# Loading and projecting the first feature block in two token halves, on one Trainium2 core

## The chip, the cores and the metric

The kernel runs on one core of one Trainium2 chip. The core has TensorE (PE, the matrix engine, with its weight loads listed apart as PEld), VectorE (DVE), ScalarE (ACT), GpSimd (POOL) and SyncE (SP, which here issues most DMAs). The metric is the device time of one execution in microseconds (us), the median over several executions; lower is better.

## The reference

One inference step of a two-layer decoder, for 1024 prompt tokens and 8 x 4 sample tokens (1056 columns together), model width 1024. Only the first token mixer, a causal convolution module, matters here:

```python
hn = rms_norm(h, norm_mix_pre)
a, g = split(hn @ w_glu + b_glu, 2)     # w_glu is 1024 x 2048
u = a * sigmoid(g)
u_ext = concatenate([prev, u])          # prev: 30 rows of state for each sample
c = depthwise_causal_conv(u_ext, w_dw) + b_dw      # width 31
m = silu(layer_norm(c)) @ w_out + b_out
```

After it come a gated FFN with a depthwise convolution of width 3, a layer with stick-breaking attention (over a paged cache of 4096 positions for the samples), and a second FFN.

## The kernel before

Everything is held feature-major: features on the 128 partitions in KB = 8 blocks, the T = 1056 tokens along the free dimension (TT = 8 prompt tiles of 128 tokens and one sample tile of 32). The order of work on each engine is written out by hand, one function for each engine and stage, and engines wait for each other on counting semaphores; each engine runs its list in order, so an instruction that waits holds all behind it.

Each fp32 product is made of three fp32r products. An operand x is cast to its high part on ACT (`xh`), and DVE subtracts to get the low part (`xl`); a weight tile `raw` gives `whi` (ACT, `split_hi`, L341) and `wlo` (DVE, `split_lo`, L345) in the same way. PE adds whi\*xh, whi\*xl and wlo\*xh in PSUM.

The load stage (`load_sp`, `load_pe`, `load_act`, `load_dve`) does this for all 1056 tokens at once. SP loads the token tiles, the first weight tile, the state rows (`srow`), the FFN state rows (`frow`) and the second weight tile. PE turns each token tile (L394) and DVE copies it out of PSUM to `hT` (L471). ACT squares each tile and takes roots; DVE spreads the inverse roots over a diagonal (L479, L483), PE multiplies by a matrix of 1/D to broadcast them (`scales`, L404), and ACT copies them to `rs` (L448): one half of NH = 528 tokens from the first five tiles, the other when all tiles are in. PE turns the state rows (L425) and the FFN rows (L1397), which ACT copies out (L752, L464). Then, for each feature block k, DVE scales `hT` to `xl32` (L509), ACT casts it to `xh` (L458) and DVE makes `xl` (L506).

The GLU stage (`glu_pe`, `glu_act`, `glu_dve`, ...) goes over eight output blocks m, each with a gate product (b = 0) and a value product (b = 1). Block 0 is `first_pair` (L633): its contraction steps k are taken as the operands come, the value two steps behind the gate:

```python
                for k in range(KB + 2):
                    if k < KB:
                        block(0, k)
                    if k >= 2:
                        block(1, k - 2)
```

Each step is nine matmuls of 352 columns. `quad_taps_spread` (L601, L605) follows, then blocks 1 to 7 (L566, and L587 for the last block in halves). ACT reads a block's gate through a sigmoid (L800) and its value (L808). For each of blocks 0 to 6 DVE forms u (L901), sums 29 taps of the convolution in place (L916) and joins the tap sums that PE made (L941); ACT makes the first two taps (L823, L824) and, ahead of them in block 0, the convolution's weight matrices (`quad_weights`, L745, 32 small instructions). `last_gate` (L818) is block 7's sigmoid.

## Time and profile before

| | before |
|---|---|
| median of 3 executions | 3124.04 us (3123.03 to 3125.28) |
| the profiled execution, its own time | 3125.5 us |
| its span | 3123.8 us |
| mean granted TensorE clock | 0.995 |
| PE busy | 3082.4 us (99%) |
| DVE busy | 1982.5 us (63%) |
| ACT busy | 1380.9 us (44%) |
| DMA, mean over the span | 171 GB/s |

Times in the trace count from the start of the span. "Busy" of PE is modelled for pipelined matmuls: one matmul's duration overlaps the next, so the pace is read from starts, not from durations. The profiled execution took 1.7 us more than its span and 1.5 us more than the median.

### The profile page before, as it was taken

The page shows a single profiled execution, that of the slowest core. Times are in us where ns is not written, and L with a number is a line of the kernel's source. Part 1 is how long each engine was busy: PE and PEld are TensorE (multiplying, and loading weights), DVE is VectorE, ACT ScalarE, POOL GpSimd, SP SyncE. Part 2 cuts the span into 40 slices and gives each one's busy share as a digit, 9 for nine tenths or more (in the row PEclk, how much of TensorE's full clock was granted, in tenths as well). Part 3 has the DMA queues.
Part 4 walks back from the last instruction along what each step waited for, and adds up shares of the span by engine and source line. Part 5 has one row for each costly group of instructions (what it writes and reads, how often), then busy time and mean ns, then how long its engine had stood idle before and what let it go on. Part 6 is the DMA issues. An engine that isn't in the chain of part 4 may idle for free.

```text
span 3123.8 us, 68300 instructions
## 1 busy us (share of the span) xinstructions
PE 3082.4 (99%) x27784; PEld 2805.0 (90%) x27784; DVE 1982.5 (63%) x2987; ACT 1380.9 (44%) x2350; POOL 230.0 (7%) x424
## 2 busy tenths in 40 slices
PE   8999999999999999999999999999999999999998
PEld 7988999999999999999666666666799999999998
DVE  6998677644665445543777877777566763465533
ACT  5445633233333333323767677776543223333322
POOL 0211000000000002321111111011000000000000
PEclk9999999999999999999999999999999999999999
DMA  4223233333333335547999999999523333333332
GB/s 129 81 74 82 82 95 88 88 99 109 113 97 87 99 111 175 191 148 222 352 390 383 380 380 386 387 393 371 201 88 89 88 95 101 111 112 86 95 111 84
DMA packets 483067, 535.14 MB, mean 171 GB/s; under 512 B 22673, under 2 KB 401162, under 8 KB 482552
## 3 DMA queue, kind: packets, MB, share of 16 engines
q1 hardware_dynamic: 467254, 482.83, 46.0%
q0 software_dynamic: 15408, 47.75, 4.6%
q8 instruction: 221, 3.62, 0.5%
q14 instruction: 92, 0.75, 0.1%
q10 hardware_dynamic: 92, 0.19, 0.0%
HBM read 486.90 MB, written 33.95 MB: 167 GB/s over the span
## 4 chain that ended last, share of the span: by engine, by line
PE 88%; DVE 8%; ACT 2%; issue 2%; DMA 1%; SPq 0%; DVEq 0%; POOL 0%; ACTq 0%; POOLq 0%
PE PS L1103 60%; PE PS L2168 8%; PE PS L2204 4%; PE PS L2181 4%; DVE mT L916 4%; PE PS L2219 3%; PE PS L2229 2%; PE PS L2238 2%; DVE wlo L345 1%; PE PS L2190 1%; PE PS L633 1%; ACT whi L341 1%; PE PS L1714 1%; PE PS L986 0%; PE PS L677 0%
## 5 line engine op out<-in xcount | busy, mean ns | idle before, releaser
L345 DVE TENSOR_TENSOR wlo<-raw,whi 128x1024 fp32r<-128x1024 f32 x368 | 450.4, 1224 | 574.7 <-ACT whi L341 561.4
L341 ACT CAST whi<-raw 128x1024 fp32r<-128x1024 f32 x368 | 386.1, 1049 | 963.3 <-PE PS L1103 923.6
L1103 PE MATMUL PS<-xfh,whi 128*128 128x264 f32 (+1 forms) x3072 | 631.1, 287 | 0.9 <-DVE wlo L345 0.9
L1103 PE MATMUL PS<-xfl,whi 128*128 128x264 f32 (+1 forms) x3072 | 625.4, 285 | 0.0
L1103 PE MATMUL PS<-xfh,wlo 128*128 128x264 f32 (+1 forms) x3072 | 624.0, 284 | 0.0
L1103 PEld LDWEIGHTS PS<-xfh,whi 128*128 128x128 f32 x3072 | 479.3, 188 | 4.5 <-issue 1.7
L1103 PEld LDWEIGHTS PS<-xfl,whi 128*128 128x128 f32 x3072 | 478.9, 188 | 0.0
L1103 PEld LDWEIGHTS PS<-xfh,wlo 128*128 128x128 f32 x3072 | 478.2, 188 | 0.0
L1103 PE MATMUL PS<-pA,whi 128*128 128x264 f32 x2048 | 333.0, 284 | 0.0
L1103 PEld LDWEIGHTS PS<-pA,whi 128*128 128x128 f32 x2048 | 282.4, 188 | 0.4
L2168 PE MATMUL PS<-ident,kr 128*128 128x128 f32 x2048 | 276.6, 276 | 0.2 <-ACT kt L2299 0.2
L2168 PEld LDWEIGHTS PS<-ident,kr 128*128 128x128 f32 x2048 | 225.9, 140 | 46.2 <-issue 45.5
L2379 DVE COPY kt<-PS 128x512 f32<-128x512 f32 x256 | 170.2, 678 | 104.8 <-PE PS L2168 104.3
L1103 PE MATMUL PS<-pA,wlo 128*128 128x264 f32 x1024 | 205.7, 282 | 0.0
L2299 ACT COPY kt<-PS 128x512 f32<-128x512 f32 x256 | 152.2, 595 | 49.7 <-PE PS L2168 46.7
L1519 DVE TENSOR_SCALAR cv<-gx,fT 128x528 f32<-128x528 f32 (+2 forms) x132 | 49.5, 403 | 189.4 <-issue 182.4
L1103 PEld LDWEIGHTS PS<-pA,wlo 128*128 128x128 f32 x1024 | 157.5, 188 | 0.0
L1523 DVE SCALAR_TENSOR_TENSOR cv<-gx,fT,cv 128x528 f32<-128x528 f32 (+2 forms) x264 | 142.4, 581 | 3.1
L2204 PE MATMUL PS<-vr,wT 128*32 128x256 f32 x2048 | 137.5, 385 | 2.8 <-ACT wT L2316 1.5
L916 DVE SCALAR_TENSOR_TENSOR mT<-u,vec,mT 128x513 f32<-128x513 f32 (+1 forms) x203 | 135.9, 749 | 4.4 <-ACT mT L823 4.4
L1461 ACT ACTIVATE gel<-cv 128x528 f32<-128x528 f32 x88 | 56.9, 646 | 184.3 <-DVEq L1530 184.3
L2181 PE MATMUL PS<-kt,qst 128*32 128x512 f32 x1024 | 124.3, 600 | 5.3 <-issue 3.8
(351 smaller groups left out, 5058.9 us busy)
## 6 DMA issues: line engine op xcount, KB each, us to landing
kr<-in_cache_k SPq DMA_DIRECT2D x256, 512.0 KB, 6.5
vr<-in_cache_v SPq DMA_DIRECT2D x256, 512.0 KB, 6.4
raw<-in_ffn_w_gate SPq DMA_DIRECT2D x88, 512.0 KB, 3.8
raw<-in_ffn_w_up SPq DMA_DIRECT2D x88, 512.0 KB, 3.8
raw<-in_ffn_w_down SPq DMA_DIRECT2D x64, 512.0 KB, 4.1
raw<-in_ffn_w_down SPq DMA_DIRECT2D x32, 384.0 KB, 3.3
raw<-in_conv_w_glu SPq DMA_DIRECT2D x16, 512.0 KB, 4.1
raw<-in_conv_w_out SPq DMA_DIRECT2D x16, 512.0 KB, 4.1
```

What stands on the lines that cost most here:

```text
L341: nc.scalar.copy(whi[b][:], raw[b][:]).then_inc(w_hi, 1)
L345: nc.vector.tensor_tensor(wlo[b][:], raw[b][:], whi[b][:].bitcast(F32), ALU.subtract).then_inc(w_lo, 1)
L916: glu_then(nc.vector.scalar_tensor_tensor(out=d, in0=src, scalar=w, in1=d, op0=ALU.mult, op1=ALU.add))
L1103: mm = nc.tensor.matmul(PS[:, s + c, 0:c1 - c0], wt[t % RING][:, kw + k, :], x(k0 + k)[:, c0:c1], start=start and k == 0 and wt is whi and ...
L1523: then(nc.vector.scalar_tensor_tensor(out=d, in0=win(j), scalar=tap, in1=s_, op0=ALU.mult, op1=ALU.add))
L2168: mm = nc.tensor.transpose(PS[:, bank, j * P:(j + 1) * P], kr[slot][:, a * P:(a + 1) * P], ident[:])
L2181: mm = nc.tensor.matmul(PS[32 * g:32 * g + 32, 2, :], qst[:, c // SEQ_CHUNKS, a, :], kt[:, a, :], start=e == 0, stop=e == 1, skip_group_ch ...
L2204: mm = nc.tensor.matmul(PS[32 * g:32 * g + 32, 3, 0:256], wT[c % 2][:, m, 32 * g:32 * g + 32], vr[slot][:, 256 * g:256 * g + 256], start=F ...
L2219: mm = nc.tensor.matmul(PS[:, 4 + hh, 0:w], qp[pr % 2][r, i * P:(i + 1) * P], kp[pr % 2][r, 512 * kc:512 * kc + w], start=True, stop=True)
L2229: mm = nc.tensor.transpose(PS[:, bank, j * P:(j + 1) * P], wq[hh][:, j * P:(j + 1) * P], ident[:])
L2299: nc.scalar.copy(kt[:, 0:4, m * P:(m + 1) * P], PS[:, turn_bank("page", x, 0), :].rearrange("p (a s) -> p a s", a=4)).then_inc(s_ka, 1)
L2379: nc.vector.tensor_copy(kt[:, 4:8, m * P:(m + 1) * P], PS[:, turn_bank("page", x, 1), :].rearrange("p (a s) -> p a s", a=4)).then_inc(s_kd, 1)
```

## The change

Token tiles arrive in the order 0 to 6, samples, 7; the second weight tile is asked for right behind the first, ahead of the state rows. The operands of block 0 are made in two halves of 528 tokens: sixteen scalings, casts and subtractions of 528 columns instead of eight of 1056. Half 0 needs only the first five tiles and the scales made from them; tile 7's copy to `hT` and the second inverse roots stand on DVE between steps 4 and 5 of half 0. `first_pair(h)` makes gate and value of one half with 264-column matmuls (six for each step) in PSUM banks 4h to 4h+3. The second scales product, the two turns of the state rows and the turn of the FFN rows are taken out of the load and put inside `first_pair(0)`. ACT reads block 0 in halves (`first_half`) and its table switch comes later. The small DVE work for the convolution weights (`wz`, `pick4`) moves behind the operands. `quad_taps_spread` uses bank 3 instead of 7. The remaining edits renumber semaphore counts.

```diff
+        X_ORDER = (0, 1, 2, 3, 4, 5, 6, TT, TT - 1)
+
         def load_sp(sp):
-            for t in range(TT):
-                sp.dma_start(xtok[:, t, :], A["x_prompt"][0][t * P:(t + 1) * P, :]).then_inc(ld_x[t], 16)
-            sp.dma_start(xtok[0:NS, TT, :], A["x_sample"].rearrange("b q d -> (b q) d")).then_inc(ld_x[TT], 16)
+            for t in X_ORDER:
+                if t < TT:
+                    sp.dma_start(xtok[:, t, :], A["x_prompt"][0][t * P:(t + 1) * P, :]).then_inc(ld_x[t], 16)
+                else:
+                    sp.dma_start(xtok[0:NS, TT, :], A["x_sample"].rearrange("b q d -> (b q) d")).then_inc(ld_x[TT], 16)
             sp.wait_ge(ld_x[6], 16)
             load_tile(sp, 0, 0, cols(w_glu, KB), KB)
+            load_tile(sp, 1, 1, cols(w_glu, 0), KB)
...
             ffn_rows_dma(sp, 0, frow0)
...
-        X_AFTER = (None, None, None, None, 1, 2, 3, 5, 6)
+        X_BANK = (4, 6, 0, 2, 6, 0, 2, 6, 4)
+        X_AFTER = (None, None, None, None, 1, 2, 3, 4, None)
+
+        def scales_pe(pe, part):
...
-                pe.wait_ge(x_rt, 3 + r)
...
-                        mm = nc.tensor.transpose(PS[:, 4 + 2 * r + k % 4 // 2, c0:c0 + 120], srow[:, j, k * P:(k + 1) * P], ident[0:120, 0:120])
-                mm.then_inc(st_pe, 1)
-            pe.wait_ge(tr_v, TT + 1)
-            ffn_rows_pe(pe, 0, frow0, 3)
+            scales_pe(pe, 0)
+            turned(EARLY + 2)
+            turned(EARLY + 3)
...
-            scales_out(0)
+            for i, t in enumerate(X_ORDER):
+                n = P if t < TT else NS
+                act.wait_ge(ld_x[t], 16)
+                if i == TT:
+                    act.wait_ge(x_sq, i)
+                    scales_out(0)
+                elif i >= 2:
+                    act.wait_ge(x_sq, i - 1)
+                j = i % 2 if i < TT else 1
+                nc.scalar.activation(junk[j][0:n, :], xtok[0:n, t, :], ACT.Square, accum_out=ssum[0:n, t:t + 1]).then_inc(x_sq, 1)
+                for a, b in ((0, EARLY), (EARLY, TT + 1)):
+                    if i == b - 1:
+                        act.wait_ge(x_sq, b)
+                        nc.scalar.activation(std[:, a:b], ssum[:, a:b], ACT.Sqrt, bias=eps_k[:, 0:1], scale=2.0 ** -30).then_inc(x_rt, 1)
+
+            def high(h, k):
+                act.wait_ge(n_t, KB * h + k + 1)
+                c = slice(h * NH, h * NH + NH)
+                nc.scalar.copy(xh[:, k, c], xl32[:, k, c]).then_inc(n_hi, 1)
+
+            split_hi(act, 0, 0, 0)
+            for k in range(KB):
+                if k == KB - 1:
+                    act.wait_ge(tr_pe, TT + 1)
+                high(0, k)
+                if k == 1:
+                    split_hi(act, 1, 0, 1)
+                if k == 5:
+                    scales_out(1)
+            state_rows_out(act, 0)
+            high(1, 0)
+            state_rows_out(act, 1)
+            high(1, 1)
+            act.wait_ge(f_st, 1)
+            nc.scalar.copy(fT[:, :, :], PS[:, 4, 0:19 * FB].rearrange("p (f r) -> p f r", f=FB)).then_inc(f_ft, 1)
+            for k in range(2, KB):
+                high(1, k)
             table("sigmoid_and_others")
-            split_hi(act, 0, 0, 0)
-            scales_out(1)
-            state_rows_out(act, 0)
-            act.wait_ge(g_wz, 2)
-            for k in range(KB):
-                act.wait_ge(n_t, k + 1)
-                nc.scalar.copy(xh[:, k, :], xl32[:, k, :]).then_inc(n_hi, 1)
-                if k == 0:
-                    split_hi(act, 1, 0, 1)
-                if k == 1:
-                    state_rows_out(act, 1)
-                    act.wait_ge(f_st, 1)
-                    nc.scalar.copy(fT[:, :, :], PS[:, 3, 0:19 * FB].rearrange("p (f r) -> p f r", f=FB)).then_inc(f_ft, 1)
 
...
+            turned(EARLY + 2)
...
+            dve.wait_ge(x_rt, 2)
+            dve.wait_ge(x_sq, TT)
+            scaled(0, 0)
+            scaled(0, 1)
+            split_lo(dve, 0, 0)
+            low(0, 0)
+            for k in range(2, KB):
+                scaled(0, k)
+                if k == 3:
+                    split_lo(dve, 1, 1)
+                low(0, k - 1)
+                if k == 4:
+                    turned(EARLY + 3)
+                    inverse_roots(1, EARLY, TT + 1)
+            dve.wait_ge(x_rt, 4)
+            scaled(1, 0)
+            low(0, KB - 1)
+            for k in range(1, KB):
+                scaled(1, k)
+                low(1, k - 1)
+            low(1, KB - 1)
             dve.wait_ge(g_wz, 1)
...
+                    if k == 0 and h == 1:
+                        pe.wait_ge((f_ft, st_a)[b], b + 1)
                     if b == 0:
-                        pe.wait_ge(n_lo, k + 1)
+                        pe.wait_ge(n_lo, KB * h + k + 1)
                     for wt, x in ((whi, xh), (whi, xl), (wlo, xh)):
-                        for c, (c0, w) in enumerate(CH):
-                            mm = nc.tensor.matmul(ps(b, c, w), wt[b][:, k, :], x[:, k, c0:c0 + w],
+                        for c in range(2):
+                            c0 = h * NH + CW2 * c
+                            mm = nc.tensor.matmul(PS[:, 4 * h + 2 * b + c, 0:CW2], wt[b][:, k, :], x[:, k, c0:c0 + CW2],
                                                   start=k == 0 and wt is whi and x is xh, stop=k == KB - 1 and wt is wlo)
                     if k == KB - 1:
-                        mm.then_inc(w_used, 1)
+                        mm.then_inc((g_h0, w_used)[h], 1)
 
                 for k in range(KB + 2):
                     if k < KB:
                         block(0, k)
                     if k >= 2:
                         block(1, k - 2)
-
-            pe.wait_ge(x_rt, 4)
-            first_pair()
+                    if h == 0 and k == 5:
+                        scales_pe(pe, 1)
+                    if h == 0 and k == 7:
+                        state_rows_pe(pe, 0)
+                    if h == 0 and k == 8:
+                        state_rows_pe(pe, 1)
+                if h == 0:
+                    pe.wait_ge(st_a, 1)
+                    ffn_rows_pe(pe, 0, frow0, 4)
+
+            first_pair(0)
+            first_pair(1)
...
+            def first_half(h):
+                c = slice(h * NH, h * NH + NH)
+                if h == 1:
+                    act.wait_ge(w_used, 3)
+                else:
+                    act.wait_ge(g_h0, 2)
+                nc.scalar.activation(two(sig[:, c]), PS[:, 4 * h:4 * h + 2, 0:CW2], ACT.Sigmoid,
+                                     bias=vec[:, 0, V_BGLU + 1:V_BGLU + 2]).then_inc(g_sig, 1)
+                if h == 1:
+                    act.wait_ge(w_used, 4)
+                nc.scalar.activation(two(val[:, c]), PS[:, 4 * h + 2:4 * h + 4, 0:CW2], ACT.Identity,
+                                     bias=vec[:, 0, V_BGLU:V_BGLU + 1]).then_inc(g_ev, 1)
+
+            first_half(0)
             split_hi(act, 2, 1, 0)
-            gate(0)
-            value(0)
...
-            act.wait_ge(st_a, 2)
             act.wait_ge(x_sp, 3)
-            nc.scalar.copy(wq4[:].rearrange("p g m j -> p (g m j)"), PS[:, 7, 0:P]).then_inc(g_wr, 1)
+            nc.scalar.copy(wq4[:].rearrange("p g m j -> p (g m j)"), PS[:, 3, 0:P]).then_inc(g_wr, 1)
             act.wait_ge(cst, 2)
-            nc.scalar.copy(wq7[0:96].rearrange("p g j -> p (g j)"), PS[0:96, 7, P:P + 4 * TAP8])
```

On ACT, in the load stage, this stood before (`xh<-xl` casts of `xl32`; `scaled` is counted up by DVE's scalings, `load_spread` by PE's broadcast products, `load_states_transposed` by PE's turns of the state rows):

```order
L448 COPY rs<-PS 128x528 [waits load_spread]
L719 ACT_TABLE_LOAD
L341 CAST whi_176<-raw_174 128x1024 [waits weights_used,weights_landed0]
L448 COPY rs<-PS 128x528 [waits load_spread]
L752 COPY stA<-PS 128x480 [waits load_states_transposed]
L752 COPY stA<-PS 128x480
L458 CAST xh<-xl_61 128x1056 [waits scaled,glu_paired_taps]
L341 CAST whi_177<-raw_175 128x1024 [waits weights_used,weights_landed1]
L458 CAST xh<-xl_61 128x1056 [waits scaled]
```

and this stands there now:

```order
L466 CAST xh<-xl_61 128x528 [waits scaled] x4
L446 COPY rs<-PS 128x528 [waits load_spread]
L466 CAST xh<-xl_61 128x528 [waits scaled]
L466 CAST xh<-xl_61 128x528 [waits scaled,transposed]
L806 COPY stA<-PS 128x480 [waits load_states_transposed]
L806 COPY stA<-PS 128x480
L466 CAST xh<-xl_61 128x528 [waits scaled]
L806 COPY stA<-PS 128x480 [waits load_states_transposed]
L806 COPY stA<-PS 128x480
L466 CAST xh<-xl_61 128x528 [waits scaled]
L482 COPY fT<-PS 128x418 [waits ffn_rows_transposed]
L466 CAST xh<-xl_61 128x528 [waits scaled] x6
```

The copy of the second scales (L446) now stands between the casts of steps 5 and 6 of half 0, and the copies of the state rows and FFN rows stand around the first two casts of half 1.

On PE, around the second scales product in half 0, now (`scaled_lo` is counted up by DVE when a step's `xl` is made, `load_diagonal` by its spread inverse roots):

```order
L678 MATMUL PS<-xh,whi_177 128x264 x2
L678 MATMUL PS<-xl,whi_177 128x264 x2
L678 MATMUL PS<-xh,wlo_179 128x264 x2
L397 MATMUL PS<-spread,mean_198 128x264 [waits transposes_read_dve,load_diagonal]
L397 MATMUL PS<-spread,mean_198 128x264
L678 MATMUL PS<-xh,whi_176 128x264 [waits scaled_lo]
```

Before, that product (L404), the turns and block 0 stood on PE one after the other. The product now comes after steps 0 to 5 of half 0's gate and 0 to 3 of its value.

On PE, at the seam between the halves, now:

```order
L409 MATMUL PS<-ident,srow 128x120 [waits load_root,state_rows_landed]
L409 MATMUL PS<-ident,srow 128x120 x7
L678 MATMUL PS<-xh,whi_177 128x264 x2
L678 MATMUL PS<-xl,whi_177 128x264 x2
L678 MATMUL PS<-xh,wlo_179 128x264 x2
L1463 MATMUL PS<-ident,frow_62 128x19 [waits ffn_rows_landed0,load_states_read]
L1463 MATMUL PS<-ident,frow_62 128x19 x21
L678 MATMUL PS<-xh,whi_176 128x264 [waits scaled_lo,ffn_rows_read]
```

The turns of the state rows stand before the last two value steps of half 0, the turn of the FFN rows behind them, and half 1's first matmul waits until ACT has copied the FFN rows out (`ffn_rows_read`).

## Rows read from the trace of the kernel before

**Rows 1.** Chain of waits, 0 to 110 us: start, us, what.

```profile
17.14 8.22 DMA sbias<-in_sb_bias
...
25.41 3.46 PE PS L425 x16
28.87 2.46 PE PS L1397 x22
31.33 25.90 PE PS L633 x144
...
68.68 6.72 DVE mT L916 x10
```

**Rows 2.** Windows: stretch, length, busy us of PE, PEld, DVE, ACT, POOL, granted clock, DMA share, GB/s.

```profile
22.00:24.00 2.00, 1.64 (x4) 0.83 (x4) 1.53 (x3) 0.52 (x1) 0.00 (x0) 0.70 1.10 211
...
31.30:36.50 5.20, 5.20 (x18) 4.84 (x18) 5.20 (x6) 3.39 (x5) 0.00 (x0) 0.50 0.33 101
36.50:57.20 20.70, 20.70 (x134) 20.48 (x136) 12.06 (x11) 6.71 (x8) 0.00 (x0) 1.00 0.03 8
237.65:241.28 3.63, 3.63 (x17) 3.63 (x18) 3.55 (x7) 0.54 (x1) 1.71 (x4) 0.53 0.75 203
```

**Rows 3.** Timeline of PE, 0 to 60 us: start, us, what, idle before and its releaser.

```profile
17.25 1.16 PE L404 MATMUL PS<-spread,mean 128*128 128x264 f32 x4 [0.50 <-DVE spread L479]
...
22.36 1.72 PE L404 MATMUL PS<-spread,mean 128*128 128x264 f32 x4 [2.11 <-DVE spread L483]
...
31.26 1.25 PE L633 MATMUL PS<-xh,whi 128*128 128x352 f32 x3
...
41.58 0.65 PE L633 MATMUL PS<-xl,whi 128*128 128x352 f32 x3
...
56.56 0.65 PE L633 MATMUL PS<-xh,wlo 128*128 128x352 f32 x3
```

**Rows 4.** Timeline of DVE, 110 to 420 us: the same step in blocks 1 and 2.

```profile
117.16 0.75 DVE L941 SCALAR_TENSOR_TENSOR mT<-PS,vec,mT 128x512 f32<-128x512 f32 x1
...
145.14 0.75 DVE L941 SCALAR_TENSOR_TENSOR mT<-PS,vec,mT 128x512 f32<-128x512 f32 x1
```

**Rows 5.** Timeline of PE, 225 to 300 us.

```profile
237.65 0.65 PE L587 MATMUL PS<-xh,whi 128*128 128x264 f32 x2 [2.34 <-ACT sig L818]
...
240.74 0.64 PE L587 MATMUL PS<-xl,whi 128*128 128x264 f32 x2
...
263.94 0.41 PE L587 MATMUL PS<-xl,whi 128*128 128x264 f32 x2
...
269.30 0.40 PE L587 MATMUL PS<-xh,wlo 128*128 128x264 f32 x2
```

**Rows 6.** Timeline of ACT, 0 to 110 us.

```profile
20.18 1.28 ACT L719 ACT_TABLE_LOAD   x1
21.48 1.04 ACT L341 CAST whi<-raw 128x1024 fp32r<-128x1024 f32 x1
...
57.25 1.44 ACT L808 ACTIVATE val<-PS,vec 128x352 f32<-128x352 f32 x3 [1.93 <-PE PS L633]
```

**Rows 7.** The tile `raw` (weights as loaded), 0 to 60 us: DMA from issue to landing.

```profile
DMA to landing us min/median/max: 3.8/4.8/9.4
```

**Rows 8.** Groups by form: line, engine, what, shapes, count | busy us, mean ns | idle before.

```profile
L471 DVE COPY hT<-PS 128x1024 f32<-128x1024 f32 x8 | 9.7, 1219 | 8.9 <-PE PS L394 8.6
...
L345 DVE TENSOR_TENSOR wlo<-raw,whi 128x1024 fp32r<-128x1024 f32 x3 | 3.7, 1222 | 6.9 <-ACT whi L341 6.9
...
L448 ACT COPY rs<-PS 128x528 f32<-128x528 f32 x2 | 1.2, 588 | 1.6 <-PE PS L404 1.6
...
L479 DVE TENSOR_TENSOR spread<-ident,std 128x384 f32<-128x384 f32 x1 | 0.6, 559 | 0.0
...
L1055 DVE TENSOR_TENSOR xl<-xl,xh 128x528 fp32r<-128x528 f32 x8 | 5.7, 708 | 4.4 <-ACT xh L1071 4.1
...
L1071 ACT CAST xh<-xl 128x528 fp32r<-128x528 f32 x8 | 5.1, 634 | 0.3
```

More of the change, by code:

```diff
@@ L383, in yoco_step @@
         EARLY = 5
-        X_BANK = (4, 6, 0, 2, 6, 0, 2, 0, 2)
-        X_AFTER = (None, None, None, None, 1, 2, 3, 5, 6)
+        X_BANK = (4, 6, 0, 2, 6, 0, 2, 6, 4)
+        X_AFTER = (None, None, None, None, 1, 2, 3, 4, None)
+        def scales_pe(pe, part):
+            pe.wait_ge(x_dg, part + 1)
+            pe.wait_ge(tr_v, (1, TT)[part])
+            if part == 0:
+                pe.wait_ge(g_wz, 1)
+            for c in (2 * part, 2 * part + 1):
+                mm = nc.tensor.matmul(PS[:, 4 + c, 0:CW2], mean1[:], spread[:, CW2 * c:CW2 * c + CW2], start=True, stop=True)
+            mm.then_inc(x_sp, 1)
@@ new lines, in state_rows_pe @@
+        def state_rows_pe(pe, r):
+            pe.wait_ge(ld_s, 48)
+            if r == 0:
+                pe.wait_ge(tr_v, TT + 1)
+            else:
+                pe.wait_ge(x_rt, 4)
+            for k in range(4 * r, 4 * r + 4):
+                for j in range(2):
+                    c0 = (k % 2) * 240 + j * 120
+                    mm = nc.tensor.transpose(PS[:, 4 + 2 * r + k % 4 // 2, c0:c0 + 120], srow[:, j, k * P:(k + 1) * P], ident[0:120, 0:120])
+            mm.then_inc(st_pe, 1)
@@ L395, in turned @@
                                              xtok[0:n, t, k * P:(k + 1) * P], ident[0:n, 0:n])
                 mm.then_inc(tr_pe, 1)
-            def scales(part):
-                pe.wait_ge(x_dg, part + 1)
-                pe.wait_ge(tr_v, (1, EARLY)[part])
-                if part == 0:
-                    pe.wait_ge(g_wz, 1)
-                for c in (2 * part, 2 * part + 1):
-                    mm = nc.tensor.matmul(PS[:, 4 + c, 0:CW2], mean1[:], spread[:, CW2 * c:CW2 * c + CW2], start=True, stop=True)
-                mm.then_inc(x_sp, 1)
@@ L407, in load_pe @@
             pe.wait_ge(cst, 2)
-            for t in range(EARLY + 1):
-                turned(t)
+            for i in range(EARLY + 1):
+                turned(i)
             pe.wait_ge(ld_v, LD_V)
@@ L493, in load_dve, with scaled, low @@
             turned(EARLY + 1)
+            turned(EARLY + 2)
+            def scaled(h, k):
+                c = slice(h * NH, h * NH + NH)
+                nc.vector.scalar_tensor_tensor(out=xl32[:, k, c], in0=hT[:, k, c], scalar=vec[:, k, V_MIX_PRE:V_MIX_PRE + 1],
+                                               in1=rs[:, c], op0=ALU.mult, op1=ALU.mult).then_inc(n_t, 1)
+            def low(h, k):
+                c = slice(h * NH, h * NH + NH)
+                dve.wait_ge(n_hi, KB * h + k + 1)
+                nc.vector.tensor_tensor(xl[:, k, c], xl32[:, k, c], xh[:, k, c].bitcast(F32), ALU.subtract).then_inc(n_lo, 1)
+            dve.wait_ge(x_rt, 2)
[19 more added lines that the diff above has]
+            low(1, KB - 1)
             dve.wait_ge(g_wz, 1)
```

111 lines of the change are left out of this document (44 added, 67 removed).

## The prediction

> **What bounds the kernel now.** I read the chain of waits over the first 110 us first, to see which engine holds the end of each stretch. The landing of the state rows and the head bias ends at 25.36, PE turns the state rows and the FFN rows, and block 0's 144 matmuls run without a break until 57.23 [rows 1]. So block 0 starts at 31.3 although its operands could have been there before: the turns stand ahead of it, and they wait for a DMA. Then the windows, for TensorE's clock. It falls to 1.2 GHz shortly before 23, when PE had stood nearly idle, and the first 5.2 us of block 0 run at that level; from 36.5 on it is 2.4 GHz [rows 2]. The timeline of PE gives the idle stretch before the fall, 2.11 us, and the pace: from 41.58 to 56.56 lie 31 groups of three 352-column matmuls, so 161 ns each [rows 3].
>
> What must not be overlooked is what carries the time from 57 on. The taps of block 0 on DVE start only at 68.68 [rows 1], 11.45 us behind the end of block 0's product, because ACT has to read the value, cast a weight tile and make 32 tap matrices first. After that DVE repeats a block every 27.98 us (117.16 to 145.14) [rows 4], and at the end of the stage PE stands 2.34 us waiting for a sigmoid that waits for DVE [rows 5]. So the gain or loss of this change is the shift of the end of block 0's product, plus what changes in those 11.45 us. All later work hangs on that DVE chain and moves with it; a shift is kept in full.
>
> **The change, part by part.** I follow the three engines through their new lists, with each time a start of the span plus durations of rows, and look for the end of block 0, which was 57.23.
>
> *Start of half 0.* PE's first scales product ends where it did, about 18.4 [rows 3], and ACT copies it in 0.6 us. ACT then has tile 7's square and a root left; the whi cast, at 21.48 before, had a table load of 1.28 us ahead of it [rows 6] that is now later, so it starts about 20.5. Its DMA, issued at the old place, would have landed by then (it was issued at 15.6, and 4.8 us is the median) [rows 7]. DVE scales two steps (20.5 to 21.2), makes wlo (1.22 us) [rows 8], then xl of step 0, at 23.4. PE starts at **23.5**, 7.8 us sooner.
>
> *Half 0 runs at DVE's pace.* A 528-column subtraction takes 708 ns and starts of neighbours lie some 0.08 closer; with a scaling of like size a step costs 1.30 us on DVE. Up to xl of step 5 there are five such steps, plus a weight subtraction (1.22), tile 7's copy (1.22), and the small root and the spreading (0.56 and its neighbours, some 0.9 together) [rows 8]: ready at 33.1. For its part PE needs 12 matmuls for a step of both products, 1.46 us at 2.4 GHz; the pace of 264-column matmuls is 122 ns there (263.94 to 269.30, 44 of them) and 221 ns at 1.2 GHz (237.65 to 240.74, 14 of them) [rows 5]. I take the first eight us at 1.2 GHz, as PE stood 3.4 us before. This costs little here, since PE waits for DVE anyway (1.1 us before step 2): PE is through its ten blocks at about 35.2.
>
> *First new wait.* Now the second scales product, 1.0 us. ACT's copy of it (0.6) ends at 37.1, and in ACT's list it stands ahead of the casts of steps 6 and 7. DVE has scaled both long before and stands waiting for xh of step 6, from 33.8 to 37.8; xl of step 6 is there at 38.4. PE waits from 36.2 to 38.5: **2.3 us**.
>
> *Second new wait.* Six blocks of half 0 are left (6 x 6 x 0.122 = 4.4), with the two turns of the state rows and that of the FFN rows between and behind. These took 3.46 and 2.46 us at 1.2 GHz [rows 1]; at 2.4 GHz they cost between half and all of that, and I take 2.0 and 1.8, nearer half for the wide ones. So PE is done at 46.7. Half 1 waits until ACT has copied the FFN rows out (0.5 and the latency): **0.85 us**, so it starts at 47.6. Its operands are a close second: ACT's casts of half 1 stand behind these copies, but xl of steps 0 to 2 are ready by 48.6, ahead of their use, and later ones stay ahead. State and FFN rows have landed long before (25.36 for what came before the second weight tile; some 2 us later now, still far ahead of 41).
>
> *Half 1.* 96 matmuls at 122 ns are 11.7 us, and 0.2 for the last one to drain: block 0 ends at **59.5**, 2.3 us later than before. In sum: start 23.5, work 28.2 (192 x 0.122 = 23.4; 1.0; 3.8), waits 1.1 + 2.3 + 0.85, low clock 3.3 and drain 0.2. Before: start 31.3, work 23.2 (144 x 0.161), low clock 2.3 (the 5.2 us took 18 matmuls), the rest gaps and drain. So the head start of 7.8 us is spent on 4.8 us of turns and scales that now lie inside, 4.2 of waits and 1.0 of clock.
>
> *The clock in the first new wait.* A PE idle stretch of 2.11 and one of 2.34 us each ended in the fall to 1.2 GHz [rows 3, 5]. The new one of 2.3 us is of that size. The stretch behind the later one lasted 3.6 us [rows 2]; 16 matmuls of 221 instead of 122 ns make **1.5 us**, and I take it. The bounds are 0, and 2.3 for 5.2 us as at block 0's start.
>
> *Behind block 0.* ACT had three value reads of 352 columns after the last matmul (1.44 us, from 57.25) [rows 6]; now it has one of 528 left, about 0.7. Everything behind it on ACT is the same, so the DVE taps come **0.7 us** sooner after block 0. PE's own part does not gain, so its wait of 2.34 us at the end of the stage shrinks to 1.7; the 1.2 GHz stretch behind it may vanish, worth 0 to 1.6 us; I take 0. The sample tile's earlier place, bank 3, and the renumbered counts cost nothing: PE and DVE wait elsewhere there. `wz` on DVE (three small operations) ends at 55, before anybody asks.
>
> *Splitting the matmuls.* 192 x 122 against 144 x 161 ns is +0.2 us, contained in the sum above. The Trainium skill's page "TensorE: Matmul & The Clock Gate", section "Back-to-back issue gap", speaks against narrower matmuls: it gives a sustained spacing of about 81 ns at 128 columns and 131 ns at 512, so that spacing hardly shrinks with width. By that, interpolated as an estimate, 192 x 99 against 144 x 110 ns is +3.1 us, 2.9 worse than the rows. The trace disagrees with it: 161 ns at 352 columns is already above its figure for 512.
>
> Sum: +2.3 + 1.5 - 0.7 = **+3.1 us**. The profiled execution would take 3125.5 + 3.1 = 3128.6 us (span 3126.9); it lies 1.5 us above the median, so the forecast is 3124.04 + 3.1 = **3127.1 us**. 0.2% is 6.2 us, about what a measurement of this kernel can tell from no change; the forecast is inside it.
>
> **The rivals.** (a) *The clock stays at 2.4 GHz.* Then +1.6, and with the late stretch gone too 0.0: 3124.0 to 3125.6. For it: the gap is just at the size of those that fell, and more work lies around it. (b) *The second weight tile lands late.* A tile took 9.4 us to land at worst [rows 7]; issued at 16.4, it would be there at 25.8 instead of the 22.4 I assume (6 us, between median and worst). It then holds ACT's cast of step 2, and block 0 ends 1.1 us later: 3128.2. (c) *Slower by over 0.2%.* TensorE falls to 1.2 GHz at 36 to 38 us and stays there, since turns did not raise it before: it was at 1.2 GHz all through the 3.46 and 2.46 us of turns and for 5.2 us of matmuls after [rows 1, 2]. Then the six blocks cost 3.6 more, the turns 2.1 and the first 5.2 us of half 1 2.3: together 8.0 on the +1.6 of (a), so +9.6 and 3133.6. It decides from the point where half 1 starts at the low level after turns at the low level. Against: here matmul blocks lie between the turns. (d) *Faster.* ACT and PE do not bite: the waits of 4.2 us and the low clock of 3.3 go, block 0 ends at 52.0, and with 0.7 this is -5.9, with the late stretch -7.5: 3116.5 to 3118.1. Against: the order of ACT's list makes the first wait certain, unless DVE is much faster than its rows. (e) *Each matmul costs the same whatever its width.* The bound is 192 x 161 ns, 7.5 over the sum: 3134.6. Against: the two paces differ as the widths do [rows 3, 5]. The Trainium skill's spacing, above, would be a mild form.
>
> **How the numbers follow.** Forecast 0.48, (a) 0.28, (b) 0.10, (c) 0.09, (d) 0.04, (e) 0.01. The range of 8 in 10 holds the forecast, (a), (b) and their bounds: 3122 to 3131. Faster is (d), 0.04; slower (c), (e), 0.10; within 0.2%: 0.86.
>
> **What would show it.** In the trace after: first 264-column matmul near 23.5; PE idle 2.3 us behind the second scales product, released by DVE's xl, which waited for ACT's cast; a short idle behind the FFN rows' turn, released by ACT's copy; the end of block 0 at 59 to 61; DVE's first tap 10.8 us behind it; blocks on DVE still every 28 us. A block 0 that ends before 55 or after 64 makes the prediction wrong.

## The result, and the profile after

The changed kernel took 3129.97 us (median of 16 runs, 3125.80 to 3133.28), the kernel before 3124.75 us on the same chip (16 runs, 3123.00 to 3128.30): ratio 1.0017, 95% interval 1.0010 to 1.0023. That is 5.2 us slower, where 3.1 was forecast; the time lies in the range given. The profiled execution took 3132.74 us with a span of 3131.0.

The chain of waits of the changed kernel, 0 to 110 us (start, us, what), has both new waits in it:

```profile
17.85 1.17 PE PS L397 x4
...
27.70 8.29 PE PS L678 x48
35.99 0.90 PE PS L397 x4
36.94 0.47 issue
37.41 0.64 ACT xh L466
38.08 0.72 DVE xl L526
38.84 4.72 PE PS L678 x24
...
46.67 1.48 PE PS L1463 x22
48.18 0.52 ACT fT L482
48.74 13.49 PE PS L678 x96
...
72.95 6.73 DVE mT L982 x10
```

The 24 matmuls at 38.84 took 4.72 us and the 96 of half 1 took 13.49; at 122 ns apiece they would be 2.9 and 11.7. The windows (columns as in [rows 2]) say why: TensorE fell to 1.2 GHz behind each of the two waits.

```profile
38.00:40.00 2.00, 1.16 (x7) 1.16 (x8) 1.92 (x3) 0.58 (x2) 0.00 (x0) 0.84 0.01 4
40.00:42.00 2.00, 2.00 (x11) 2.00 (x11) 0.76 (x2) 0.00 (x0) 0.00 (x0) 0.50 0.00 0
42.00:44.00 2.00, 2.00 (x16) 2.00 (x16) 0.00 (x0) 0.00 (x0) 0.00 (x0) 0.81 0.00 0
...
48.00:50.00 2.00, 1.40 (x11) 1.30 (x10) 1.69 (x4) 1.58 (x3) 0.00 (x0) 0.90 0.00 0
50.00:52.00 2.00, 2.00 (x11) 2.00 (x11) 2.00 (x4) 0.66 (x2) 0.00 (x0) 0.50 0.00 0
52.00:54.00 2.00, 2.00 (x14) 2.00 (x14) 2.00 (x4) 1.24 (x2) 0.00 (x0) 0.75 0.00 0
```

On DVE's timeline the taps begin at 72.95 instead of 68.68, 4.3 us later [rows 1], and the blocks still come every 27.98 us (121.42 to 149.40), as in [rows 4].

```profile
72.95 6.73 DVE L982 SCALAR_TENSOR_TENSOR mT<-u,vec,mT 128x513 f32<-128x513 f32 x10 [4.37 <-ACT mT L877]
...
121.42 0.75 DVE L1007 SCALAR_TENSOR_TENSOR mT<-PS,vec,mT 128x512 f32<-128x512 f32 x1
...
149.40 0.75 DVE L1007 SCALAR_TENSOR_TENSOR mT<-PS,vec,mT 128x512 f32<-128x512 f32 x1
```

At the end of the stage the picture is another. The timeline of PE shows the wait for the sigmoid shorter than in [rows 5] (1.60 instead of 2.34), and the clock stayed at 1.00 behind it. But now PE waits for a transfer, the shifted copies of block 7's first half:

```profile
241.95 0.51 PE L631 MATMUL PS<-xh,whi 128*128 128x264 f32 x2 [1.60 <-ACT sig L872]
...
253.38 7.33 PE L731 MATMUL PS<-shifted,quads 128*32 128x264 f32 x128 [1.33 <-DMA shifted<-u]
```

In the kernel before the same taps had no wait (its timeline of PE):

```profile
249.22 7.33 PE L677 MATMUL PS<-shifted,quads 128*32 128x264 f32 x128
```

The low clock had made PE late enough for them. A run described below, e8, shows it: DVE wrote its u at 239.51, where the kernel before has 239.46, the clock stayed at 1.00 behind the wait for the sigmoid, and PE then stood until the same moment for the copies.

```profile
249.28 7.33 PE L680 MATMUL PS<-shifted,quads 128*32 128x264 f32 x128 [1.48 <-DMA shifted<-u]
```

DVE's timeline of the kernel before has this for the first step on the layer norm's mean, from which on all is the same code:

```profile
263.90 2.55 DVE L1038 TENSOR_TENSOR mT<-mT,PS 128x528 f32<-128x528 f32 x4 [3.81 <-PE PS L986]
```

That step starts at 268.07 in the changed kernel, 4.2 us later. From there on single executions differ by some us: the profiled one of the changed kernel ends 7.2 us behind that of the kernel before (3132.74 against 3125.5), 4.2 of which are there at this step.

The traces place most of the other 3.0 us in the layer with attention, in code that the change does not touch. The kernel before had a fall of the clock there which the changed kernel, behind the same wait, had not. PE's timeline, of the kernel before and then of the changed one:

```profile
1493.68 3.42 PE L2181 MATMUL PS<-kt,qst 128*32 128x512 f32 x16 [1.60 <-issue]
```

```profile
1498.23 1.92 PE L2247 MATMUL PS<-kt,qst 128*32 128x512 f32 x16 [1.59 <-issue]
```

Of the fourteen profiles only that one has a fall at this place. At the end of the attention it went the other way. PE of the changed kernel waited for a transfer that PE of the kernel before did not wait for, and its clock was then low for longer (windows of the changed kernel; the kernel before has 0.72 and 1.00 in the same two):

```profile
2221.67 0.64 PE L2270 MATMUL PS<-vr,wT 128*32 128x256 f32 x8 [1.64 <-DMA vr<-in_cache_v]
```

```profile
2225.00:2230.00 5.00, 2.88 (x21) 2.78 (x20) 2.78 (x5) 3.09 (x6) 0.00 (x0) 0.50 0.38 110
2230.00:2235.00 5.00, 5.00 (x28) 5.00 (x28) 5.00 (x9) 3.42 (x7) 0.00 (x0) 0.59 0.39 101
```

On DVE the distance between the two kernels is 2.0 us ahead of this wait (2213.28 and 2215.31, the copies to `aT`), 4.9 us at the first subtractions behind it (2222.70 and 2227.65), and 6.7 us behind the low clock (2267.87 and 2274.61, the same subtraction of a weight tile). Of the other runs only e2 (1.23 us) and e3 (0.41) waited for that transfer; whether the change brings the wait about is not shown. So single profiles are compared up to the step on the mean, and times by their medians.

### The profile page after: what moved, and what is told of

The parts are those of the page before. It is cut to its first block, busy times and chain, and to the rows that moved or that the text cites. A ratio compares the mean times of both kernels' runs of the same rounds, so it can differ in the third digit from the quotient of the medians.

```text
span 3131.0 us, 68420 instructions
## 1 busy us (share of the span) xinstructions
PE 3081.6 (98%) x27832; PEld 2805.8 (90%) x27832; DVE 1985.0 (63%) x3003; ACT 1382.8 (44%) x2356; POOL 230.6 (7%) x424
## 4 chain that ended last, share of the span: by engine, by line
PE 86%; DVE 8%; ACT 2%; issue 2%; DMA 1%; SPq 0%; DVEq 0%; POOL 0%; ACTq 0%; POOLq 0%
PE PS L1169 59%; PE PS L2234 8%; PE PS L2270 4%; PE PS L2247 4%; DVE mT L982 4%; PE PS L2285 3%; PE PS L2295 2%; PE PS L2304 2%; DVE wlo L345 1%; PE PS L678 1%; PE PS L2256 1%; ACT whi L341 1%; PE PS L1780 1%; PE PS L1052 0%; PE PS L731 0%
```

## The experiments

Differences are of medians, against the kernel before on the same chip. "First tap" and "mean step" are the two starts just read, in the one profiled execution; before: 68.68 and 263.90. The kernel before took 3124.19 us beside e1 to e4, 3125.51 beside e5 to e8 and 3123.86 beside e9 to e12 (33 runs each), so the absolute times in the expectations have to be read as differences too.

| run | us | minus before | ratio, 95% interval | first tap | mean step |
|---|---|---|---|---|---|
| changed kernel | 3129.97 | +5.2 | 1.0010 to 1.0023 | 72.95 | 268.07 |
| e1 | 3128.71 | +4.5 | 1.0000 to 1.0018 | 70.62 | 267.96 |
| e2 | 3129.33 | +5.1 | 1.0009 to 1.0027 | 71.29 | 266.17 |
| e3 | 3131.92 | +7.7 | 1.0013 to 1.0032 | 70.40 | 268.64 |
| e4 | 3124.51 | +0.3 | 0.9991 to 1.0009 | 66.94 | 262.28 |
| e5 | 3131.01 | +5.5 | 1.0012 to 1.0030 | 70.69 | 266.09 |
| e6 | 3128.92 | +3.4 | 1.0002 to 1.0020 | 67.99 | 263.05 |
| e7 | 3126.80 | +1.3 | 0.9996 to 1.0014 | 66.00 | 263.71 |
| e8 | 3124.88 | -0.6 | 0.9993 to 1.0011 | 68.69 | 263.96 |
| e9 | 3123.62 | -0.2 | 0.9990 to 1.0008 | 68.18 | 263.14 |
| e10 | 3121.62 | -2.2 | 0.9981 to 0.9999 | 68.12 | 261.83 |
| e11 | 3128.29 | +4.4 | 1.0001 to 1.0019 | 73.33 | 267.30 |
| e12 | 3122.37 | -1.5 | 0.9987 to 1.0005 | 66.50 | 260.38 |

An interval is about 3 us to each side (2 us for the changed kernel), and the ratio is not that of the two medians: its middle lies up to 1.7 us from their difference. So neighbours in the table can't be told apart by it; the traces have to do it.

### e1: the scales copy behind the casts

```
-                if k == 5:
-                    scales_out(1)
+            scales_out(1)
```

The new line stands behind the loop over the casts.

> The changed kernel with one edit: ACT copies the second scales after the casts of steps 6 and 7 of half 0, not before them. Theory (the waits for each other in the new lists, and the fall of TensorE's clock behind them, cost the time): PE's 1.96 us behind the scales product goes, the 1.2 GHz stretch of 39.3 to 42.7 goes with it (1.5 us), block 0 ends near 58.7 instead of 62.2, and the time falls by 3 to 3.5 us against the changed kernel, to about 3126.5. Rival 1 (DVE is the limit, and the wait only moves): half 1 gets its operands later, block 0 ends at 61 or after, under 1.5 us gained. Rival 2 (low clock comes whatever the waits are): 2 us gained, a 1.2 GHz stretch between 36 and 48 remains.

Of the first wait 0.7 us was left (PE was busy 3.33 of 4 us from 36 to 40), and no low clock came there; the one behind the second wait stayed (0.50 in 48 to 50 us). The taps began 2.3 us earlier than in the changed kernel. Yet the mean step gained only 0.1 and the median 0.7 (3 to 3.5 were expected), and the timeline of PE and the windows show where the rest went: a longer wait for the transfer and a fall of the clock behind it.

```profile
251.59 9.02 PE L730 MATMUL PS<-shifted,quads 128*32 128x264 f32 x128 [1.86 <-DMA shifted<-u]
```

```profile
250.00:252.00 2.00, 0.41 (x7) 0.19 (x11) 2.00 (x4) 1.98 (x5) 1.43 (x3) 0.92 0.06 19
252.00:254.00 2.00, 2.00 (x24) 1.06 (x20) 2.00 (x5) 1.11 (x1) 0.17 (x1) 0.50 0.21 62
254.00:256.00 2.00, 2.00 (x32) 1.01 (x28) 2.00 (x5) 0.00 (x0) 0.00 (x0) 0.72 0.00 0
```

### e2: the FFN rows' turn behind block 1's gate

```
-                if h == 0:
-                    pe.wait_ge(st_a, 1)
-                    ffn_rows_pe(pe, 0, frow0, 4)
...
+                if m == 0:
+                    pe.wait_ge(g_ev, 2)
+                    ffn_rows_pe(pe, 0, frow0, 7)
```

The first of these places is the end of half 0. ACT copies the rows out behind `states_in(2)`, and half 1 no longer waits for that copy.

> The changed kernel with the turn of the FFN rows (22 small transposes) and ACT's copy of them moved from the seam of the two halves to behind block 1's gate product; half 1 no longer waits for the copy. Theory: 1.5 us of turns, the 0.6 us wait and the 1.2 GHz stretch at 49.6 to 53.0 (1.5 us) leave the path; the turn is free where it goes, as PE has 1.6 us of wait on DVE at the end of the stage. Block 0 ends near 58.6, time 3 to 3.6 us below the changed kernel. Rival 1: PE is the bound after block 0 as well, then 1.5 us come back as later work and only 2 remain. Rival 2: half 1's operands (ACT's casts behind the state copies) are as late as the copy was, then under 1.5 us.

The second wait and its low clock were gone; the first kept both (0.57 in 40 to 44 us), and half 1 then waited for DVE's operands in pieces. The taps came 1.7 us earlier and the mean step 1.9. The median did not follow (+5.1 us against +5.2; 3 to 3.6 less were expected). This profile has the wait and the long low clock at the end of the attention too (1.23 us; 0.50 in 2225 to 2230 us).

### e3: the first wait filled with unread matmuls

```
+                        pe.wait_ge(tr_v, TT + 1)
+                        for j in range(14):
+                            nc.tensor.matmul(PS[:, 4, 0:CW2], whi[0][:, 0, :], xh[:, 0, 0:CW2], start=True, stop=True)
```

> The changed kernel with 14 matmuls of 264 columns that nobody reads (1.7 us) put behind the second scales product, into PE's wait of 1.96 us. Nothing waits less. Theory on the clock: the fall at 39.3 comes from the idle stretch, so it does not come, the matmuls behind run at 122 instead of 221 ns, block 0 ends 1.5 us sooner (60.7), time about 1.5 us lower. If the fall has another cause: no change in the clock, block 0 ends at 62.2 or some tenths later.

The operand comes no earlier (39.36, against 38.84 in the changed kernel), but PE is busy until shortly before it. The granted clock is then 1.00 in every window from 34 to 58 us, behind both waits:

```profile
38.00:42.00 4.00, 3.71 (x30) 3.51 (x30) 2.69 (x4) 1.10 (x3) 0.00 (x0) 1.00 0.01 2
...
46.00:50.00 4.00, 3.40 (x37) 3.30 (x36) 3.52 (x6) 2.43 (x5) 0.00 (x0) 1.00 0.00 0
50.00:54.00 4.00, 4.00 (x35) 4.00 (x34) 4.00 (x7) 2.01 (x4) 0.00 (x0) 1.00 0.00 0
```

The narrow matmuls and the turns are all there, so they alone do not bring a fall. That the filled wait is the reason is likely but not shown by this one execution: in e5, below, the same wait stood unfilled and the clock stayed up, and here it also stayed up behind the second wait, which nobody had filled. The chain shows the two stretches of the changed kernel at the full clock, 3.20 us instead of 4.72 and 11.95 instead of 13.49: each fall had cost 1.5 us.

```profile
39.36 3.20 PE PS L678 x24
...
47.74 11.95 PE PS L678 x96
```

The taps begin at 70.40, 2.6 us earlier than in the changed kernel. The timeline of PE also settles the pace: nine groups of two lie between these rows, 121 ns for a 264-column matmul.

```profile
39.72 0.40 PE L678 MATMUL PS<-xl,whi 128*128 128x264 f32 x2
...
41.90 0.40 PE L678 MATMUL PS<-xl,whi 128*128 128x264 f32 x2
...
252.46 8.82 PE L734 MATMUL PS<-shifted,quads 128*32 128x264 f32 x128 [2.93 <-DMA shifted<-u]
```

The last row is where the profile lost it again: 2.93 us of waiting for the transfer, and a mean step 0.6 us later than in the changed kernel. A time 1.5 us lower was expected. Why the median is the highest of all is not settled.

### e4: all casts first

```
             scales_out(1)
-            state_rows_out(act, 0)
             high(1, 0)
-            state_rows_out(act, 1)
+            state_rows_out(act, 0)
             high(1, 1)
+            state_rows_out(act, 1)
```

and e1 and e2 in one.

> Both edits of the first two runs, and ACT casts steps 0 and 1 of half 1 each before the state rows' copies instead of behind them. Theory: the savings add up, block 0 ends near 55 (at most 56), the first tap on DVE near 66, and the time is 2 to 2.5 us BELOW the kernel before the change (about 3122.3), and 7 below the changed kernel. If narrow matmuls and half-width operands cost time by themselves, this kernel still does not beat the one before. Rival (DVE the limit): block 0 ends at 57 or later, time as before the change.

With both waits gone block 0 ran at 2.4 GHz from 34 us on, the taps began 1.7 us before those of the kernel before, and the time was that of the kernel before (+0.3): these orders on ACT and PE make the difference to the changed kernel's +5.2. But 2 to 2.5 us under the kernel before were expected, and the mean step did come 1.6 us earlier than there; the median does not show it. In the tail the wait for the transfer was 1.40.

### e5 to e7: the last u earlier

```
-                    if a == 2 and m == KB - 2:
+                    if a == 1 and m == KB - 2:
                         last_u(dve, 0)
```

> Edit: the changed kernel with last_u(0) of VectorE (the half of block 7's u that the last taps need) behind the first pair of taps of block 6 instead of behind the second; nothing else. In the changed kernel TensorE has ended the turns of block 6's states at 252.05 us and waits 1.33 us for the transfers of shifted<-u, which start when that u is written (244.39). Theory A (what moves with VectorE's chain reaches the layer norm's mean through this transfer, and through nothing else): u is written 1.3 us earlier, its transfers land at 252.1, the wait at 253.38 falls to 0.0 to 0.2 us, the step on the mean starts at 266.8 instead of 268.07, and the time is 1.1 to 1.4 us under the changed kernel's: 3128.7 us (ratio to the kernel before 1.0012). Rival B (the last transfers are paced by the queues behind the shifts of block 6, or TensorE's own order sets the end): the wait stays over 1 us and the time is the changed kernel's 3130.0 within 0.5 us.

> Edit: the scales copy behind all casts of half 0 (as in the run before with that edit alone, 3128.71 us) and last_u(0) behind the first pair of taps. With the first edit alone VectorE's taps began 2.3 us earlier than in the changed kernel, but the step on the mean only 0.1 us earlier, behind a wait of 1.86 us for shifted<-u and a granted clock of 0.65 to 0.78 in 250 to 256 us. Theory A (the gain was given back to that wait and to the fall of the clock behind it): with the transfer 1.3 us earlier the wait falls to 0.3 to 0.7 us, the clock stays at 1.00, the last taps take 7.33 us instead of 9.02, the step on the mean starts at 264.9 to 265.3, and the time is 3125.7 us (3125.2 to 3126.3). Rival B (the loss has another cause, so that it comes back elsewhere): the step on the mean stays at 267 or later and the time over 3127.5.

> Edit: the version with all casts ahead of the row copies (3124.51 us, wait of 1.40 us for shifted<-u, step on the mean 262.28) and last_u(0) behind the first pair of taps. Theory A: the wait falls to about 0.1 to 0.2 us, the step on the mean starts at 261.0 and the time is 3123.2 us (3122.7 to 3123.8), ratio 0.9996 to the kernel before. Rival B (as in the first of these runs): 3124.5, unchanged.

In the first and third the rival held (+5.5 us where the changed kernel had +5.2, +1.3 where e4 had +0.3). In the second the mean step came at 263.05, but block 0 had no fall behind its waits in this execution (taps at 67.99), and the time stayed 3.4 us over the kernel before, where theory A had 1.5. The wait for the transfer did not shrink in any as A had it: 1.57, 1.19 and 2.16 us. In e7 u is written 2.1 us earlier than in e4 (235.82 against 237.90; 0.9 of it come from the taps' start), and the copies are there 0.3 us earlier (247.34 against 247.60). PE's timeline of e7, and DVE's:

```profile
247.34 9.01 PE L730 MATMUL PS<-shifted,quads 128*32 128x264 f32 x128 [2.16 <-DMA shifted<-u]
```

```profile
235.82 0.71 DVE L1027 TENSOR_TENSOR u<-val,sig 128x528 f32<-128x528 f32 x1
```

So the copies are not paced by u alone. In SP's queue the shifts of block 6 and a weight tile of 512 KB stand ahead of them.

### e8 and e9: block 0 whole, only the turns moved

From the kernel before: the DMA of the second weight tile ahead of the state rows', and

```
-            state_rows_out(act, 0)
...
+            state_rows_out(act, 0)
+            state_rows_out(act, 1)
...
+                    if k == 4:
+                        state_rows_pe(pe, 0)
+                    if k == 7:
+                        state_rows_pe(pe, 1)
```

with the copies behind the last cast, and the FFN rows' turn as in e2. e9 has `k == 5` in place of `k == 7`.

> Edit: the kernel before, its operand and block 0 whole (no halves), with three parts of the change's order alone: the second weight tile's DMA ahead of the state rows', the turns of the state rows inside block 0's products (banks 6 and 7, behind the steps 4 and 7) and their copies behind the last cast, the FFN rows' turn behind block 1's gate product. In the kernel before VectorE waits 2.04 us for the first cast, which stands on ScalarE behind the copies of the first state rows, and block 0 starts at 31.26. Theory A (halves win nothing that this order does not win as well): the first cast ends at 27.2, the first low part at 28.5, block 0 starts at 28.6, 2.7 us earlier; the sixteen turns take 2.0 us of it back inside block 0; block 0 ends 0.5 to 0.9 us earlier, at 56.3 to 56.7, and the time is 3123.4 us (3122.5 to 3124.3), at or under the version in halves with the same repairs (3124.5). Rival B (the halves are what moves the start; here the clock at 1.2 GHz covers all that is won): block 0 still ends at 57.2 or later and the time is 3124.2 to 3126.

> Edit: the whole block with the turns moved (3124.88 us beside 3125.51 of the kernel before), with the second turn of the state rows behind step 5 of block 0 instead of step 7. In that run block 0 started at 28.91 as expected, but ScalarE's second copy of state rows came at 54.08, ahead of sig and val of block 0, and val started at 57.26 as in the kernel before. Theory A (that order alone took the gain back): the copy moves to about 48.5, sig to 53.9, val starts at 56.6 to 56.9, VectorE's u at 57.6 to 57.9 instead of 58.83, the first taps 1.0 to 1.2 us earlier, and the time is 1.5 to 2.1 us under the kernel before (ratio 0.9993 to 0.9995). Rival B (a gain of block 0 is given back at the wait for shifted<-u): val is as early, but the step on the mean starts at 263.5 or later and the time is within 0.8 us of the kernel before.

Block 0 began at 28.91 and 28.65, near the 28.6 expected and 2.4 and 2.6 us before that of the kernel before. In e8 the value read began where it had been (57.26), because ACT's copy of state rows stood ahead of it; in e9 it began at 56.75. ACT's timeline, of e8 and then of e9:

```profile
54.08 1.02 ACT L755 COPY stA<-PS 128x480 f32<-128x480 f32 x2 [8.51 <-PE PS L394]
...
57.26 1.47 ACT L811 ACTIVATE val<-PS,vec 128x352 f32<-128x352 f32 x3
```

```profile
48.04 1.02 ACT L755 COPY stA<-PS 128x480 f32<-128x480 f32 x2 [2.72 <-PE PS L394]
...
56.75 1.45 ACT L811 ACTIVATE val<-PS,vec 128x352 f32<-128x352 f32 x3 [1.62 <-PE PS L629]
```

The rest of the 2.6 us went to the sixteen turns inside the products and to short waits for DVE's operands, which set the pace of the whole block's first steps. 0.5 us were left at the taps, not the 1.0 to 1.2 of e9's theory A. Both times are the kernel before's within what can be told, where e9's theory A had 1.5 to 2.1 us less. So the start won by reordering is worth as little as that won by halves.

### e10 to e12: the weight tile behind the copies

```
-                    if t < 2 * KB + 2:
+                    if t < 2 * KB + 1:
                         weights(t)
             last_shifts(sp, 0, 0)
+            weights(2 * KB + 1)
```

with the last u earlier; e10 on e9, e11 on the changed kernel, e12 on e4.

> Edit: the kernel of the first run of this job, and at the end of the linear unit two moves: the transfer of weight tile 17 (512 KB, SyncE) behind the last shifts of half 0 instead of ahead of them, and last_u(0) behind the first pair of taps. Theory A (the transfers of shifted<-u are late because they share the DMA engines with that tile, which is why u written 1.3 us earlier brought them only 0 to 0.3 us forward): they land 2 to 3 us earlier, TensorE does not wait for them (in the run with turns moved: 1.48 us), its clock stays at 1.00 in 248 to 256, and the time is 1.3 to 1.6 us under the first run's: 3.0 to 3.6 us under the kernel before. Rival B (they are paced by their sixteen issues, 0.64 us each on SyncE): the wait stays over 0.8 us and the time is the first run's within 0.6 us.

> Edit: the changed kernel with the two moves at the end of the linear unit (tile 17 behind the last shifts, last_u(0) behind the first pair of taps), nothing else. The changed kernel is 5.2 us over the kernel before; with last_u(0) alone moved it was 5.5 over. Theory A: the wait of 1.33 to 1.57 us for shifted<-u goes, and no fall of the clock comes behind it in any run, so the time is 1.4 to 2.4 us less: 2.8 to 3.8 us over the kernel before (ratio 1.0009 to 1.0012). Rival B (that wait is no part of the loss): 4.7 us over or more.

> Edit: the version in halves with all casts ahead of the row copies and the FFN rows behind block 1's gate (0.3 us over the kernel before), with the two moves at the end of the linear unit. Theory A: the step on the mean starts at 260.5 to 261.0 instead of 262.28, and the time is 1.4 to 2.0 us less: 1.1 to 1.7 us under the kernel before (ratio 0.9995). Rival B: unchanged, 0.3 us over. Against the second run of this job, which has the same tail and block 0 whole, it tells what the halves themselves are worth: by theory A 1.5 to 2.5 us slower than it, although its block 0 ends earlier, since its TensorE goes through more waits at which the clock can fall; if halves are worth their start, it is as fast.

The queue of SP, its timeline in e9 and then in e10:

```profile
238.93 0.59 SPq L333 DMA_DIRECT2D raw<-in_conv_w_out  x1
239.72 5.95 SPq L552 DMA_DIRECT2D shifted<-u  x8
```

```profile
238.83 5.18 SPq L553 DMA_DIRECT2D shifted<-u  x8
244.06 0.59 SPq L333 DMA_DIRECT2D raw<-in_conv_w_out  x1
```

What the tile did to the copies stands in the DMA issues of e7 and of e12, which differ by the tile's place alone (count, KB each, median us from issue to landing):

```profile
shifted<-u SPq DMA_DIRECT2D x8, 73.0 KB, 5.1
shifted<-u POOLq DMA_DIRECT2D x4, 73.0 KB, 4.8
```

```profile
shifted<-u SPq DMA_DIRECT2D x8, 73.0 KB, 2.8
shifted<-u POOLq DMA_DIRECT2D x4, 73.0 KB, 2.5
```

Between e9 and e10, which differ by both moves, SP's copies went from 4.3 to 2.6 us and POOL's from 3.7 to 2.5. POOL's copies suffer as SP's do, though the tile is in SP's queue alone. That agrees with what the Trainium skill says under "DMA: Bandwidth & Descriptors", section "Issuing engines are not separate DMA queues": transfers started by different engines run on the same 16 DMA engines and interleave. The wait was 0 in e10 (1.18 in e9) and e12, and 0.20 in e11, as theory A had it. The mean step came 1.3 us earlier than in e9 and 1.9 earlier than in e4. By time, e10 is 2.0 us under e9, e12 1.8 under e4, e11 0.8 nearer to the kernel before than the changed kernel, between what its two theories had. The last two differences are smaller than the intervals. For the first the single executions, eleven of each on one chip, say more: all of e10 (3120.31 to 3123.06) lie under e9's median of 3123.62. e10 is faster than both kernels (interval 0.9981 to 0.9999 against the kernel before). It is 2.2 under, where 3.0 to 3.6 were expected.

Between e10 and e12 the medians are 3121.62 and 3122.37 (theory A had 1.5 to 2.5 between them), and ten of e12's eleven executions lie above e10's median. Yet e12's taps begin 1.6 us earlier and its mean step 1.5 us earlier. In the two profiles this turns round behind the mean step: from there to the end of the execution e10 needs 2859.0 us and e12 2861.9, and at the end of the attention e12's clock is low for longer (0.66 in 2215 to 2220 and 0.66 in 2220 to 2225 us, where e10 has 0.95 and 0.71). Whether halves bring that about is open. By time, they won no more than the whole block with its turns moved.

## Why the prediction was right in its direction and short by two us

- *Start of half 0* was given as 23.5; it was 24.06 on PE's timeline, and 23.84 and 24.84 in e5 and e11, whose block 0 is the same code. In e11 the token tile that PE waited for longest could be turned 0.5 us later (11.88, not 11.37), and behind this wait of 1.67 us the clock fell to 0.50 (12 to 14 us); behind the same wait in the changed kernel it stayed at 1.00.
- *DVE's pace, the first and the second wait*: the terms for xl of step 5 add up to 33.2, not 33.1. Waits of 2.3 and 0.85 us were forecast, 1.96 and 0.60 measured, released by DVE's xl behind ACT's cast and by ACT's copy of the FFN rows, as said. The chain's rows 37.41 and 48.18 show both.
- *The turns* at 2.4 GHz took 3.1 us in the chain (0.82, 0.82 and 1.48), where I took 3.8.
- *The end of block 0* should have been 61.0 with the low stretch included; it was 62.2 (48.74 and 13.49).
- *"The clock in the first new wait"* is the step that failed, in its count and not in its mechanism or price. I priced one fall at 1.5 us, and it cost that (4.72 against 3.20 in e3). A second one came behind the second wait and cost as much (13.49 against 11.95). That wait is only 0.60 us, far below the 2.11 and 2.34 I had compared with, and I had asked only of the first wait whether the clock would fall. 1.5 for it, the 0.3 by which the blocks behind the first wait began later (38.84, not 38.5) and 0.3 that these blocks took longer (4.72, 0.73 and 0.74, where 5.9 with the fall were forecast), less the turns' 0.7 and the second wait's 0.25, are the 1.2 us by which block 0 ended later than forecast.
- The falls are not certain. In block 0 of the changed kernel's order the clock fell behind the first wait in the changed kernel, e2 and e11 and not in e5; behind the second in the changed kernel, e1, e5 and e11 and not in e6 (e3 filled the first wait, and had none). The three runs with the same block 0 began their taps at 72.95, 70.69 and 73.33. e5 gained not only by the missing fall: its clock was back at 1.00 by 28 us, that of the changed kernel only between 32 and 34, and its first wait ended 0.8 us earlier (38.08).
- The changed kernel's times spread over 7.5 us, and they go with the clock: the five slowest of the sixteen executions are the five whose mean granted clock was 0.995, the others had 0.996 and 0.997. Block 0's waits can be only part of it, as e8 and e9, whose block 0 is whole and has no such waits, spread over 6.0 and 6.4 us (e10 over 2.8).
- *Behind block 0* the taps came 10.7 us after its end; 10.8 was forecast.
- *"The 1.2 GHz stretch behind it may vanish, worth 0 to 1.6 us; I take 0."* It vanished, and 0 was right, but for a reason I didn't have: the transfer of the copies took its place.
- *"All later work hangs on that DVE chain and moves with it; a shift is kept in full."* Held for the changed kernel (4.3 at the taps, 4.2 at the mean step) and is not general. From 237 to 264 us PE is on the path, with a wait for the copies; in e1, 2.3 us won at the taps left 0.1 at the mean step. From the first tap to the mean step it took 194.9 to 195.4 us in the kernel before, the changed kernel and e2, e4, e5, e6, e8 and e9. It took 197.3 to 198.2 where the clock fell behind that wait (e1, e7, e3), and 193.7 to 194.0 with the tile behind the copies (e10, e11, e12).
- *Rival (a)*, a clock that stays up, is what e3 built: its taps came 2.6 us earlier, not far from the 3.1 of two falls, but its time was not lower. *Rival (b)* did not occur, nor did *rival (d)*: both waits came and block 0 ended at 62.2, not 52.0. *Rival (c)*, low into half 1, did not either: between the two falls the clock was 1.00. *Rival (e)* fell with the 121 ns. The Trainium skill's spacing ("TensorE: Matmul & The Clock Gate", section "Back-to-back issue gap") would have made about 99 ns of it, by the interpolation in the prediction; the runs do not show it.
- The comparison's median is 5.2 us over the kernel before; the profile's own 4.2 us at the mean step lie inside its interval (3.1 to 7.2). Waits and clock at the end of the attention differ between executions by more than the 1 us that is left, so it can lie there, but no run here shows it.

## What to carry to other kernels

A change that starts an engine earlier and then has it wait for small copies in the middle spends the gain twice: once in the wait, once in the clock that may fall behind it; so count the waits, and price a fall for each, also for the short ones, as a chance rather than a yes or no. Before a head start is built by splitting the work, look whether reordering the copies ahead of it gives the same: here the whole block with its turns moved was by time as good as the halves. And where a shift is said to be kept, follow it to the next place at which another engine joins the path, and ask what else is under way when its transfer starts.

## What was not expected of the hardware

- The wait of 0.60 us behind the FFN rows' turn was followed by 1.2 GHz in four of five runs (the changed kernel, e1, e5 and e11, not e6), while in e3, with the same second wait but the first one filled, the clock stayed at 1.00.
- At the end of the stage the clock fell behind waits of 1.86, 2.16 and 2.93 us (e1, e7, e3) and not behind those of 0.20 to 1.57 (e11, the changed kernel, e2, e4, e5, e6, e8 and e9).
- At the sigmoid's wait it fell behind 2.34 us (kernel before) and not behind 0.99 to 1.94 (all others; 1.94 in e8). In the attention it fell behind a wait of 1.60 us in one of fourteen profiles with 1.59 or 1.60 there: the length of a wait alone does not tell whether the clock falls.
- One transfer of 512 KB issued just ahead of sixteen of some 73 KB made these land about 5 instead of 2.5 to 2.8 us after their issue (medians, e7 and e12), those from the other queue too.
